# The 32 sample rows' hi and lo parts as one stationary operand of 64 columns, in a hybrid decoder trunk

## What is computed

```python
def decoder_layer(x, ...):                       # x: 2048 prompt rows, or 32 sample rows
    h = rms_norm(x, g_mix_pre)
    z = h @ w_in                                 # 1024 -> 2048
    y_a = pool_mixer(z[..., :256], ...)          # four mixers of width 256
    y_b = conformer_conv(z[..., 256:768], ...)
    y_c = chunk_spatial_gating(z[..., 768:1280], ...)
    y_d = short_gated_conv(z[..., 1280:], ...)
    o = concatenate([y_a, y_b, y_c, y_d]) @ w_out        # 1024 -> 1024
    x = x + rms_norm(o, g_mix_post)
    f = rms_norm(x, g_ffn_pre)
    f = square(relu(f @ w_up)) @ w_down                  # 1024 -> 4096 -> 1024
    return x + rms_norm(f, g_ffn_post)
```

## Time and profile before

| | us |
|---|---|
| median of 3 runs | 2216.18 |
| lowest, highest | 2215.36, 2216.53 |
| the profiled execution | 2217.42 |
| its span, first to last instruction | 2215.5 |

### The profile page before, as it was taken

The page is one execution under the profiler, slowest core; times in us unless marked ns, Lnnn a source line. Parts: engine busy times, 40 slices in busy tenths (PEclk is TensorE's granted clock), DMA queues, the critical chain, the costliest instruction groups (busy, mean ns, idle before and its releaser), DMA issues.

```text
span 2215.5 us, 33006 instructions
## 1 busy us (share of the span) xinstructions
PE 2125.0 (96%) x14425; PEld 1935.7 (87%) x14425; DVE 1083.3 (49%) x1406; ACT 754.5 (34%) x1160; POOL 107.4 (5%) x190
## 2 busy tenths in 40 slices
PE   6999999996999999999999999999999989999997
PEld 5887777786799898989899898989899989999997
DVE  3686877867623334553333336433333553334334
ACT  4424232233432324443322334332324433314132
POOL 2011111110000000000000000000000000000000
PEclk9999999997999999999999999999999999999999
DMA  7744656463232233444332244533233333222231
GB/s 251 276 179 172 219 183 222 171 200 124 79 123 96 96 96 114 159 146 134 95 96 96 95 134 155 171 99 97 94 102 124 108 115 105 86 86 77 77 96 41
DMA packets 184836, 287.42 MB, mean 130 GB/s; under 512 B 5967, under 2 KB 162292, under 8 KB 176484
## 3 DMA queue, kind: packets, MB, share of 16 engines
q1 hardware_dynamic: 160868, 169.99, 24.0%
q0 software_dynamic: 22784, 114.28, 14.7%
q10 hardware_dynamic: 1040, 1.05, 0.1%
HBM read 245.01 MB, written 40.57 MB: 129 GB/s over the span
## 4 chain that ended last, share of the span: by engine, by line
PE 84%; DVE 7%; ACT 4%; issue 2%; DMA 2%; POOL 0%; ACTq 0%; POOLq 0%; DVEq 0%
PE mm L1795 27%; PE mm L1797 27%; PE mm L1796 27%; DVE w_lo L1144 2%; ACT w_hi L687 2%; DMA mixc<-mixT_scratch 1%; DVE conv L1188 1%; PE tr L1800 1%; DMA raw<-in_w_in 1%; PE tr L2024 1%; ACT junk_y L986 0%; PE tr L1821 0%; DVE o_sb L1479 0%; PE mm L1855 0%; DMA x_in<-in_x_prompt 0%
## 5 line engine op out<-in xcount | busy, mean ns | idle before, releaser
L1144 DVE TENSOR_TENSOR w_lo<-raw,w_hi 128x2048 fp32r<-128x2048 f32 x152 | 348.4, 2292 | 688.3 <-ACT w_hi L687 688.3
L1795 PE MATMUL mm<-act_hi,w_hi 128*128 128x512 f32 (+2 forms) x1728 | 632.7, 366 | 11.3 <-DVE act_lo L1501 6.0
L1797 PE MATMUL mm<-act_hi,w_lo 128*128 128x512 f32 (+2 forms) x1728 | 632.2, 366 | 0.0
L1796 PE MATMUL mm<-act_lo,w_hi 128*128 128x512 f32 (+2 forms) x1728 | 626.7, 363 | 0.0
L1795 PE MATMUL mm<-w_hi,u_hi 128*128 128x256 f32 (+1 forms) x2176 | 603.1, 277 | 1.6
L1796 PE MATMUL mm<-w_lo,u_hi 128*128 128x256 f32 (+1 forms) x2176 | 600.8, 276 | 0.0
L1797 PE MATMUL mm<-w_hi,u_lo 128*128 128x256 f32 (+1 forms) x2176 | 600.8, 276 | 0.0
L687 ACT ACTIVATE w_hi<-raw 128x2048 fp32r<-128x2048 f32 x152 | 290.8, 1913 | 575.5 <-PE mm L1797 568.8
L1795 PEld LDWEIGHTS mm<-w_hi,u_hi 128*128 128x128 f32 (+1 forms) x2176 | 398.3, 183 | 4.9 <-DVE u_lo L1517 3.8
L1796 PEld LDWEIGHTS mm<-w_lo,u_hi 128*128 128x128 f32 (+1 forms) x2176 | 398.3, 183 | 1.2
L1797 PEld LDWEIGHTS mm<-w_hi,u_lo 128*128 128x128 f32 (+1 forms) x2176 | 398.3, 183 | 0.7
(11 more groups left out here) (245 smaller groups left out, 1343.4 us busy)
## 6 DMA issues: line engine op xcount, KB each, us to landing
raw<-in_w_ffn_up SPq DMA_DIRECT2D x64, 1024.0 KB, 5.4
raw<-in_w_ffn_down SPq DMA_DIRECT2D x64, 1024.0 KB, 5.2
w_hi<-whi_scratch POOLq DMA_DIRECT2D x24, 1024.0 KB, 5.2
w_lo<-wlo_scratch POOLq DMA_DIRECT2D x24, 1024.0 KB, 7.9
raw<-in_w_out SPq DMA_DIRECT2D x16, 1024.0 KB, 5.2
whi_scratch<-w_hi POOLq DMA_DIRECT2D x8, 1024.0 KB, 8.9
wlo_scratch<-w_lo POOLq DMA_DIRECT2D x8, 1024.0 KB, 10.9
mixc<-mixT_scratch POOLq DMA_DIRECT2D x16, 512.0 KB, 5.7
```

What stands on the lines that cost most here:

```text
L1144: DVE.tensor_tensor(w_lo[:, s, :, :], raw[:, s, :, :], w_hi[:, s, :, :].bitcast(fp32), ALU.subtract)\
L1795: PE.matmul(out, whi, xhi, start=(k == 0), stop=False)
L1796: PE.matmul(out, whi, xlo, start=False, stop=False)
L1797: return PE.matmul(out, wlo, xhi, start=False, stop=(k == K - 1))
```

## The change

For the small groups the hi and the lo part of the sample rows lie side by side in one tile of 64 columns for each k (`smp_h` for the input panels, `smp` for output and down panels). `sample_two` takes the place of `three` there: one matmul has all 64 columns as stationary operand and `w_hi` moving, so that rows 0 to 31 of the bank get hi·hi and rows 32 to 63 get lo·hi; a second has only the 32 hi columns, with `w_lo` moving, into rows 0 to 31. A group is 16 matmuls. The two groups of bank rows are summed outside TensorE: who took the result before now takes rows 0 to 31, and then VectorE adds rows 32 to 63 (`add_part`). ScalarE signals its copy with `part_in`, VectorE its own first step with `part_sum`; `zs_ready` and `bank_free` are now raised by the added instruction. In block 0 the sum of input panel k (`zs_add(k)`) stands ahead of `split_lo(k + 2)` for k = 0 to 5. In the up panels of block 3 `u_parts` writes the sample rows by two further VectorE instructions for each k, 32 columns each.

```diff
+            sums = itertools.count(1)
+            def add_part(dst, bank, done):
+                DVE.tensor_tensor(dst, bank[NS:2 * NS, 0:PC], dst, ALU.add).then_inc(done, 1)
+            def zs_add(jj):
+                dve.wait_ge(part_in, jj + 1)
+                add_part(zs[:, COLS[jj]:COLS[jj] + PC], mm[4 + jj % 2], zs_ready)
...
             def zs_part(jj):
                 act.wait_ge(zs_done, jj + 1)
-                SC.activation(zs[:, COLS[jj]:COLS[jj] + PC], mm[4 + jj % 2][0:NS, 0:PC], ACT.Copy).then_inc(zs_ready, 1)
+                SC.activation(zs[:, COLS[jj]:COLS[jj] + PC], mm[4 + jj % 2][0:NS, 0:PC], ACT.Copy)\
+                  .then_inc(part_in, 1)
...
                 else:
+                    zs_add(0)
                     split_lo(2)
+                    zs_add(1)
                     split_lo(3)
...
                     taps(b, range(19, 22))
+                    if b == 0:
+                        zs_add(6)
                     for i in range(NCH):
                         h_lo(NCH * (b + 1) + i)
                         if i < 3:
                             tap(b, 22 + i)
+                    if b == 0:
+                        zs_add(7)
...
             def o_copy(j, i):
...
+                if tile == NCH:
+                    dst = o_sb[0:n, tile, p * PC:(p + 1) * PC]
+                    DVE.tensor_copy(dst, mm[bank][0:n, 0:PC]).then_inc(part_sum, 1)
+                    dve.wait_ge(part_sum, next(sums))
+                    add_part(dst, mm[bank], bank_free[bank])
+                    return
...
             def u_parts(j, i):
...
-                DVE.tensor_copy(u_hi[:, k, c0:c1], square[:, at % 2, 0:c1 - c0]).then_inc(u_hi_ready, 1)
+                e = min(c1, N1)
+                rest = square[:, at % 2, e - c0:c1 - c0]
+                if c1 > e:
+                    DVE.tensor_copy(smp[:, k, 0:NS], rest)
+                DVE.tensor_copy(u_hi[:, k, c0:e], square[:, at % 2, 0:e - c0]).then_inc(u_hi_ready, 1)
                 dve.wait_ge(u_hi_ready, at + 1)
+                if c1 > e:
+                    DVE.tensor_tensor(smp[:, k, NS:2 * NS], rest, smp[:, k, 0:NS].bitcast(fp32), ALU.subtract)
...
             def d_add(j, i):
...
+                if tile == NCH:
+                    dst = f2_sb[0:n, tile, p * PC:(p + 1) * PC]
+                    if q > 0:
+                        DVE.tensor_tensor(dst, mm[bank][0:n, 0:PC], dst, ALU.add).then_inc(part_sum, 1)
+                        dve.wait_ge(part_sum, next(sums))
+                    else:
+                        dve.wait_ge(part_in, NI + p + 1)
+                    add_part(dst, mm[bank], bank_free[bank])
+                    return
...
+            def sample_two(bank, x, whi, wlo, k):
+                if k < K - 1:
+                    PE.matmul(bank[0:2 * NS, 0:PC], x[:, k, :], whi, start=(k == 0), stop=False)
+                last = PE.matmul(bank[0:NS, 0:PC], x[:, k, 0:NS], wlo, start=False, stop=False)
+                if k == K - 1:
+                    last = PE.matmul(bank[0:2 * NS, 0:PC], x[:, k, :], whi, start=False, stop=True)
+                return last
...
-                            last_mm = three(mm[4 + s][0:NS, 0:PC], act_hi[:, k, N1:NX], act_lo[:, k, N1:NX],
-                                            w_hi[:, s, k, :], w_lo[:, s, k, :], k)
+                            last_mm = sample_two(mm[4 + s], smp_h, w_hi[:, s, k, :], w_lo[:, s, k, :], k)
...
+                                if tile == NCH:
+                                    last_mm = sample_two(mm[bank], smp, w_hi[:, s, k, :], w_lo[:, s, k, :], k)
+                                    continue
```

More of the change, by code:

```diff
@@ L1 @@
+import itertools
 import concourse.bass as bass
@@ L123, in hybrid_trunk_step @@
         bias2 = sb("bias2", [P, 2, P])
+        ps = ExitStack()
+        smp = sb("smp", [P, K, 2 * NS], f32r, to=ps)
+        ps.close()
         sgu_bb = sb("sgu_bb", [P, PC])
@@ L191, in hybrid_trunk_step @@
         st_out = sb("st_out", [HC, 3, GW], to=p1)
+        ps = ExitStack()
+        smp_h = sb("smp_h", [P, K, 2 * NS], f32r, to=ps)
+        ps.close()
         gs_tok = sb("gs_tok", [NS, GW], to=p1)
@@ L364, in hybrid_trunk_step @@
         y_last = sem("y_last")
+        part_in = sem("part_in")
+        part_sum = sem("part_sum")
         OUT_SMALL = 2 + 3 * NB_S + 1 + 3
@@ L774, in _ @@
             act.wait_ge(smp_tr, 1)
[L775 removed]
+            SC.activation(smp_h[:, :, 0:NS], tr[0][:, 0:K * NS].rearrange("p (k t) -> p k t", k=K), ACT.Copy)\
               .then_inc(smp_hi, 1)
@@ L909, in mix_part @@
                     wait_panel(act, index("U", b - 1, Q - 1, NP - 1))
-                SC.activation(act_hi[:, :, t0:t0 + n], mixc[:, m % 2, :, 0:n], ACT.Copy).then_inc(mix_hi, 1)
+                dst = smp[:, :, 0:NS] if i == NCH else act_hi[:, :, t0:t0 + n]
+                SC.activation(dst, mixc[:, m % 2, :, 0:n], ACT.Copy).then_inc(mix_hi, 1)
             def o_squares(j, i):
@@ L977, in d_copy @@
                               mm[bank][0:n, 0:nt * PC].rearrange("p (h c) -> p h c", h=nt), ACT.Copy)\
-                  .then_inc(bank_free[bank], 1)
+                  .then_inc(part_in if tile == NCH else bank_free[bank], 1)
             def y_squares(j, i):
@@ L1410, in _ @@
                 else:
+                    zs_add(2)
                     split_lo(4)
@@ L1417, in _ @@
                 else:
+                    zs_add(3)
                     split_lo(5)
@@ L1422, in _ @@
                 else:
+                    zs_add(4)
                     split_lo(6)
@@ L1426, in _ @@
                 if b == 0:
+                    zs_add(5)
                     split_lo(7)
@@ L1448, in mix_part @@
                 dve.wait_ge(mix_hi, m + 1)
-                DVE.tensor_tensor(act_lo[:, :, t0:t0 + n], mixc[:, m % 2, :, 0:n],
-                                  act_hi[:, :, t0:t0 + n].bitcast(fp32), ALU.subtract).then_inc(mix_lo, 1)
+                hi, lo = act_hi[:, :, t0:t0 + n], act_lo[:, :, t0:t0 + n]
+                if i == NCH:
+                    hi, lo = smp[:, :, 0:NS], smp[:, :, NS:2 * NS]
+                DVE.tensor_tensor(lo, mixc[:, m % 2, :, 0:n], hi.bitcast(fp32), ALU.subtract).then_inc(mix_lo, 1)
             def o_copy(j, i):
@@ L1514, in u_parts @@
                     dve.wait_ge(out_small, 16 * OUT_SMALL)
-                DVE.tensor_copy(u_hi[:, k, c0:c1], square[:, at % 2, 0:c1 - c0]).then_inc(u_hi_ready, 1)
+                e = min(c1, N1)
[3 more added lines that the diff above has]
+                DVE.tensor_copy(u_hi[:, k, c0:e], square[:, at % 2, 0:e - c0]).then_inc(u_hi_ready, 1)
                 dve.wait_ge(u_hi_ready, at + 1)
-                DVE.tensor_tensor(u_lo[:, k, c0:c1], square[:, at % 2, 0:c1 - c0], u_hi[:, k, c0:c1].bitcast(fp32),
+                if c1 > e:
+                    DVE.tensor_tensor(smp[:, k, NS:2 * NS], rest, smp[:, k, 0:NS].bitcast(fp32), ALU.subtract)
+                DVE.tensor_tensor(u_lo[:, k, c0:e], square[:, at % 2, 0:e - c0], u_hi[:, k, c0:e].bitcast(fp32),
                                   ALU.subtract).then_inc(u_lo_ready, 1)
@@ L1525, in d_add @@
                 f2 = f2_sb[0:n, tile:tile + nt, p * PC:(p + 1) * PC]
-                if q == 1:
-                    before = index("D", b, 0, p)
-                else:
-                    before = index("D", b, q - 1, p)
-                old, _, free = bank_of[before, i]
-                dve.wait_ge(bank_free[old], free + 1)
-                wait_bank(dve, j, i)
+                if q > 0:
+                    old, _, free = bank_of[index("D", b, q - 1, p), i]
+                    dve.wait_ge(bank_free[old], free + 1)
+                wait_bank(dve, j, i)
+                if tile == NCH:
+                    dst = f2_sb[0:n, tile, p * PC:(p + 1) * PC]
+                    if q > 0:
+                        DVE.tensor_tensor(dst, mm[bank][0:n, 0:PC], dst, ALU.add).then_inc(part_sum, 1)
[4 more added lines that the diff above has]
+                    return
                 DVE.tensor_tensor(f2, mm[bank][0:n, 0:nt * PC].rearrange("p (h c) -> p h c", h=nt), f2, ALU.add)\
@@ L1577, in d_piece @@
             def d_piece(j, i):
-                if order[j][2] > 0:
+                if order[j][2] > 0 or token_banks(order[j][1])[i][0][0] == NCH:
                     d_add(j, i)
```

5 lines of the change are left out of this document (2 added, 3 removed).

## The result

The changed kernel took 2198.78 us (median of 4 runs, 2196.90 to 2200.01), the kernel before, beside it, 2216.36 (2215.36 to 2216.67). The ratio is 0.992, with a 95% interval of 0.9907 to 0.9932: 17.6 us less, where the prediction had 21.7. The profiled execution took 2197.92 us, its span is 2196.0.

What follows compares the result with a forecast made beforehand. TensorE, with work for 96% of the span, was taken to bound the kernel. Savings of 5.8 + 2.7 + 13.2 = 21.7 us took the profiled 2217.42 us to 2195.7, the median 2216.18 to 2194.5; range 2191 to 2200.5.

Steps and rivals of the forecast that it cites:

- rival one: Wider idle gaps before block 1's transposes and output panel 1 cost clock: 3.4 us more, 2197.9 us; chance 0.11.
- Block 0: Eight input panels: shift of 5.03 us by the transposes, 0.78 us from group 7, together 5.8 us saved.
- Group 7: Block 0's last small group, after the last transposes: on the path, saves 0.78 us, block 1 starting some 0.05 us after h_lo.
- Output panels: Four output panels of block 3: group 0 saves nothing, groups 1 to 3 save 2.72 us; 2.7 us in all.
- group 0 saves nothing and the idle time becomes 1.69 us: Block 3, output panel 0 to 1: panel 1's weight split sets the start, so idle time grows from 0.78 us.
- No DMA is moved: Whole kernel: transfers stay where they are; weight stores and loads follow the splits and come sooner with them.
- Down panels and end: Block 3's sixteen down panels: fifteen groups save 13.61 us, the sixteenth nothing, the end costs 0.44 us; 13.2 us in all.
- The term of 0.907 us for a group: Each small group: 8 matmuls removed at 113.3 ns each, the remaining ones keeping the old pace.
- The `u_parts` margin: Before each first down panel: 0.49 us of margin covers 0.2 to 0.37 us added; otherwise 0.1 us lost in four places.
- Two: All 28 small groups pay, as what TensorE waits for moves too: 25.0 us saved, 2191.2 us; chance 0.03.
- three: In small groups each change of width stops the array, 163 ns each: slower, about 2250 us; chance 0.06.
- Four: In small groups each change of width costs 20 to 60 ns, 7 to 21 us: 2201 to 2215 us; chance 0.06.

Runs made afterwards that it cites:

- e1: The changed kernel unaltered, run and traced once more: 2200.00 us, ratio 0.9929 to the kernel before.
- e3: Changed kernel with the split of output panel 1's weights moved ahead of the sample rows' mixer part on ScalarE and VectorE: 2193.48 us, ratio 0.9901.
- e7: Changed kernel with block 0's input panels back at 24 matmuls of 32 columns, their sums left off VectorE: 2202.00 us, ratio 0.9943.
- e9: Changed kernel with 128 TensorE instructions (waits on an already set semaphore) added in block 1: 2197.92 us, ratio 0.9912.
- e2: Changed kernel with the second matmul of each pair also taking all 64 columns, so adding lo·lo: 2199.04 us, ratio 0.9922.
- e5: Changed kernel with the sum of input panel 6 put behind block 1's h_lo steps on VectorE: 2198.12 us, ratio 0.9922.
- e6: Changed kernel with a third matmul put back for each k, 24 in a small group, VectorE's added work kept: 2218.34 us, ratio 1.0018.
- e10: Changed kernel with output panel 1's weights split early and block 3's sample columns kept in the last columns of u_hi: 2193.66 us, ratio 0.9895.
- e12: Changed kernel with output panel 1's weights split early, 32 bytes ahead of each sample tile, panel 6's sum behind the h_lo: 2193.43 us, ratio 0.9897.

## Why the prediction was right, and where it was short

The measured 2198.78 us lie inside the range of 2191 to 2200.5, and the way each place limits the gain was right but for one. The gain was short by a fifth, and e1's median of 2200.00 is near the range's upper end, which had been set to take in rival one. By its own steps, with the mean of the two traces of the changed kernel against the one of before:

- **Block 0** (5.8 us forecast): 5.23, from 109.72 to 104.48. Six groups gave 5.14, not 5.44, by the slower pace. The transposes came forward by 4.68 (forecast 5.03), VectorE setting the time as the step said, with 3.38 us of idle time. Group 7 then gave 0.55 instead of 0.78. Its own pace was not the limit: its last matmul started at 145.75 and the last h_lo ended at 145.90. Block 1 started 0.15 us behind that and not 0.05, and from the first transposes to the last h_lo it took 9.33 us where it took 9.20.
- **Output panels** (2.7): the step that failed is "group 0 saves nothing and the idle time becomes 1.69 us". It became 2.65 and 2.37, and with the low clock behind it the step 0-1 grew by 2.68 and 2.24 us where it should have stayed. The chain that sets it was named rightly, but I took its length as fixed. The sentence "No DMA is moved" was wrong: two of its transfers took 6.3 us (e1: 6.1) instead of 5.2, with an instruction block that the shorter program moved beside them. That is 0.7 to 1.0 us of idle time. The rest, an estimated 1.5 to 1.6 us (the step less e3's step, the idle time and 0.27 us that e7 and e9 have besides), is rival one, given a chance of 0.11 and up to 1.7 us at this place: the clock fell after each idle time of 2.2 us or more (after, e1, e2, e5), never after 1.71 or less (before, e6, e7, e9). At 1.71 us, in e7, just the idle time of the forecast, it stayed full. Groups 1 to 3 and what lies behind gave 2.5 and 3.1 us, forecast 2.72. That this agrees is partly luck: the groups themselves gave 0.81 each, 2.4 in all, and the rest is the stretch behind, which varies by 1 us among kernels with the same code there.
- **Down panels and end** (13.2): down 0-15 gave 12.18 us instead of 13.61. The term of 0.907 us for a group measured 0.81: the group 0.84, less 0.03 by which the wide matmuls behind it run late. Its premise, that width doesn't show in the pace, is right (e10: 1.81 us); what I had not asked is whether the operand's new place shows. The end cost 0.45 and 0.47, forecast 0.44. The `u_parts` margin held: in block 3 there is no wait for `u_lo` (the first trace has five of 0.15 us and e1 ten, all before it, where the change adds nothing), and a quarter to the next takes 60.61 us where it took 61.41, 0.80 less and so as much as any other step.
- **Sum.** 0.57 (block 0) + 2.46 (step 0-1) - 0.11 (panels 1 to 3) + 1.43 (down) + 0.02 (end) = 4.4 us short, so the stretches that the change touches give 17.3 us, near the medians' 17.6. The span of the first trace was 19.5 us shorter than before and e1's 15.8: the lead in the middle and the 0.7 us ahead of S0 are in these, and e1 showed the first to be that execution's.
- **Rivals.** Two and three are out. Four, a small price for each change of width, had 20 to 60 ns for each change. The price is 4 ns for each matmul and does not come from the widths (e2, e10).

The best version, by e3, e10 and e12, takes 2193.4 to 2193.7 us, ratios 0.9895 to 0.9901; the three cannot be told apart. The early split gives nearly all of it.

## What to carry to other kernels

When a change takes work out of the bounding engine, ask of every place where that engine meets a chain of transfers how long it will now wait, and whether the wait is long enough to cost clock too: here 0.9 us of saved work turned into 2.5 us of loss, and moving one weight split ahead in two queues took them back, with the wait that had been there before. Price a matmul with the operand where it will lie, not where its like lies now. And compare stretches between fixed points of two or more traces before explaining a difference: one trace's middle was off by 2 us in one direction, the next one's by 3 in the other.
